# Second block, six turns between sublayers: the eight transposes of the second token tile in one group instead of two groups of four

## The reference

```python
def second_block(x, ...):
    for l in range(DEPTH):                                   # DEPTH = 2
        h = swiglu_ffn(rmsnorm(x, ffn1_pre_g[l]), ffn1_w_gu[l], ffn1_w_down[l])
        x = x + 0.5 * rmsnorm(h, ffn1_post_g[l])
        h = mixing_sublayer(rmsnorm(x, mix_pre_g[l]), w_in[l], ...)   # gating, pooling, attention, convolution
        x = x + rmsnorm(h, mix_post_g[l])
        h = swiglu_ffn(rmsnorm(x, ffn2_pre_g[l]), ffn2_w_gu[l], ffn2_w_down[l])
        x = x + 0.5 * rmsnorm(h, ffn2_post_g[l])
    return x

def swiglu_ffn(h, w_gu, w_down):                             # width 2816
    a, b = jnp.split(h @ w_gu, 2, axis=-1)
    return (jax.nn.silu(a) * b) @ w_down
```

## Time and profile before

| | |
|---|---|
| time of three runs, median (lowest to highest) | 1791.21 us (1790.86 to 1792.0) |
| the profiled execution: its time | 1792.04 us |
| its span, first to last instruction | 1790.3 us |
| granted TensorE clock, mean | 0.999 of full |
| PE busy | 1778.8 us, 99% of the span |
| PEld busy | 1588.6 us, 89% |
| DVE busy | 1402.9 us, 78% |
| ACT busy | 904.5 us, 51% |
| POOL busy | 219.7 us, 12% |
| read from HBM | 354.15 MB, 199 GB/s |

### The profile page before, as it was taken

One profiled execution on the slowest core, in us unless ns is written; L12 is line 12 of the kernel. 1 busy time (PEld: TensorE's weight loads), 2 busy tenths in 40 slices (PEclk: granted clock), 3 DMA queues, 4 the chain that ended last, 5 costly groups with the idle time before them and its releaser, 6 DMA issues.

```text
span 1790.3 us, 25922 instructions
## 1 busy us (share of the span) xinstructions
PE 1778.8 (99%) x10010; PEld 1588.6 (89%) x10010; DVE 1402.9 (78%) x1599; ACT 904.5 (51%) x998; POOL 219.7 (12%) x189
## 2 busy tenths in 40 slices
PE   9999999999999999999999999999999999999998
PEld 7988998889889898899898888998899898888997
DVE  7897867678869667777779987778777779987776
ACT  5564434445644444644555546444544555546443
POOL 0000000000001000000059230000000058230000
PEclk9999999999999999999999999999999999999999
DMA  9546565555556555655564556555655564555553
GB/s 315 205 157 227 188 212 209 189 215 200 187 215 222 205 196 186 214 197 194 181 204 172 183 210 217 202 196 192 223 199 197 188 203 167 186 212 205 201 197 117
DMA packets 52018, 357.43 MB, mean 200 GB/s; under 512 B 6552, under 2 KB 6688, under 8 KB 10080
## 3 DMA queue, kind: packets, MB, share of 16 engines
q1 hardware_dynamic: 47952, 341.93, 54.1%
q0 software_dynamic: 3696, 14.33, 2.7%
q10 hardware_dynamic: 288, 0.04, 0.0%
HBM read 354.15 MB, written 2.11 MB: 199 GB/s over the span
## 4 chain that ended last, share of the span: by engine, by line
PE 94%; DVE 4%; issue 1%; ACT 1%; DMA 1%; DVEq 0%; POOLq 0%; POOL 0%; SPq 0%; ACTq 0%
PE ps L245 21%; PE ps L327 13%; PE ps L335 13%; PE ps L328 13%; PE ps L251 11%; PE ps L207 3%; PE ps L208 3%; PE ps L209 3%; PE ps L225 2%; PE ps L232 2%; PE ps L226 2%; DVE w_lo L182 1%; PE ps L2917 1%; PE ps L2916 1%; PE ps L2921 1%
## 5 line engine op out<-in xcount | busy, mean ns | idle before, releaser
L182 DVE TENSOR_TENSOR w_lo<-raw,w_hi 128x2048 fp32r<-128x2048 f32 x312 | 717.4, 2305 | 208.4 <-ACT w_hi L175 208.0
L175 ACT ACTIVATE w_hi<-raw 128x2048 fp32r<-128x2048 f32 x312 | 596.1, 1912 | 424.1 <-PE ps L335 168.6
L245 PE MATMUL ps<-a,w_hi 128*128 128x512 f32 x1760 | 398.3, 379 | 0.8 <-ACT w_hi L175 0.8
L245 PEld LDWEIGHTS ps<-a,w_hi 128*128 128x128 f32 x1760 | 329.3, 189 | 46.0 <-ACT w_hi L175 1.2
L327 PE MATMUL ps<-w_hi,a 128*128 128x512 f32 x592 | 226.9, 383 | 0.0
L328 PE MATMUL ps<-w_hi,a 128*128 128x512 f32 x592 | 224.4, 379 | 0.0
L251 PEld LDWEIGHTS ps<-a,w_lo 128*128 128x128 f32 x1760 | 213.6, 192 | 5.9
L327 PE MATMUL ps<-w_hi,mix 128*128 128x512 f32 x576 | 218.7, 380 | 0.0
L328 PE MATMUL ps<-w_hi,mix 128*128 128x512 f32 x576 | 218.3, 379 | 0.0
L251 PE MATMUL ps<-a,w_lo 128*128 128x256 f32 x1760 | 214.2, 275 | 0.0
L335 PE MATMUL ps<-w_lo,a 128*128 128x512 f32 x592 | 139.8, 379 | 0.0
(11 more groups left out here) (416 smaller groups left out, 2267.2 us busy)
## 6 DMA issues: line engine op xcount, KB each, us to landing
raw<-in_w_b SPq DMA_DIRECT2D x198, 1024.0 KB, 4.9
raw<-in_w_a SPq DMA_DIRECT2D x124, 1024.0 KB, 4.9
rows<-in_post_gains POOLq DMA_DIRECT2D x6, 512.0 KB, 5.9
rows<-in_rows_a POOLq DMA_DIRECT2D x2, 1028.0 KB, 8.3
raw<-in_w_a SPq DMA_DIRECT2D x4, 512.0 KB, 7.1
rows<-in_rows_a POOLq DMA_DIRECT2D x2, 1024.0 KB, 6.9
x<-in_x SPq DMA_DIRECT2D x2, 512.0 KB, 6.0
a_gates<-bias_line POOLq DMA_DIRECT2D x2, 512.0 KB, 7.7
```

Source lines behind the costliest of these rows:

```text
L175: act.activation(k.w_hi[s], k.raw[:, s, :], ACT.Copy).then_inc(k.hi_ready, 1)
L182: dve.tensor_tensor(k.w_lo[s], k.raw[:, s, :], k.w_hi[s].bitcast(F32), ALU.subtract).then_inc(k.lo_ready, 1)
L245: pe.matmul(both, hi[:, kt, n * P:(n + 1) * P], k.a[:, :, kt, :].rearrange("p s (t n) -> p s n t", t=TT), start=kt == 0, stop=False)
```

## The change

At each turn the four blocks of the second half of the tile's transposes join the first four, and all eight stand behind the last product of tile 0:

```diff
@@ mlp @@
-                first_unit(1, 0, range(3))
-                x_transpose(l, n, 1, range(1))
-                first_unit(1, 0, range(3, 4)).then_inc(up0_done.sem, 1)
-                x_transpose(l, n, 1, range(1, 2))
+                first_unit(1, 0, range(4)).then_inc(up0_done.sem, 1)
+                x_transpose(l, n, 1)
                 first_unit(0, 1, range(4)).then_inc(k.chunk_done, 1)
@@ mixing sublayer @@
-                uv_part(1, 0, range(3))
-                x_transpose(l, 1, 1, range(1))
-                uv_part(1, 0, range(3, 4)).then_inc(uv_done.sem, 1)
-                x_transpose(l, 1, 1, range(1, 2))
+                uv_part(1, 0, range(4)).then_inc(uv_done.sem, 1)
+                x_transpose(l, 1, 1)
                 uv_part(0, 1, range(4)).then_inc(k.chunk_done, 1)
```

## The result

The changed kernel takes 1794.58 us, the kernel before beside it 1791.36 us, each the median of 22 runs: a ratio of 1.0019, interval [1.0013, 1.0025], or +3.2 us with an interval of +2.3 to +4.5. Forecast were 1795.1 us and +3.9 us. The interval leaves out zero, so the changed kernel is slower, by some 0.2%.

A forecast was written before the change was run, and what follows sets the result against it. PE was taken as the bound (94% of the chain), with the first transposes heading each turn's chain. Six turns x 0.65 us gave +3.9 us on the median 1791.21, so 1795.1 us; range 1793.3 to 1796.2.

The forecast's parts named there:

- ACT's 14.2 us: Sign: over all turns, ACT's waits for tile 1's transposes rise from 10.3 to 14.2 us.
- the 2.8 us in 10 waits for x: Sign: PEld's waits for x over all turns shrink from 3.7 us in 15 waits to some 2.8 us in 10.
- DVE's idle time before `x_low`: Sign in the second turn: it stays at 0.53 us or less; zero would mean DVE was the bound.
- one product per turn, 0.65 us: Each of six turns: one product moves in front of the first transposes, so the chain starts 0.65 us later.
- Wait for x worth nothing: In five turns PEld's 0.18 us wait for `x_new` goes, but gains 0; bounds 0 and 0.18 us a turn.
- no cost per group: At each turn, eight transposes in one group take as long as two groups of four; none saved.
- Rival 1: Exposed weight load of the transposes, 0.14 us, comes back in five turns: +3.2 us, 1794.4 us; chance 0.09.
- rival 2: Something the turn does not move sets the mixing sublayer's end, swallowing two turns' delay: +2.6 us, 1793.8 us; chance 0.12.
- the step at a mixing sublayer: Sign of rival 2: later turns' start shifts of 0.65, 1.3, 1.95, 2.6, 3.25 us would show a step there.
- Rival 3: At the turns DVE's last addition of x heads the chain, so not slower: -0.9 us, 1790.3 us; chance 0.03.
- Rival 4: Dearer: PE's clock falls in the turns, 1822 us, or mixing sublayer weight loads slow, up to 1796.2; chance 0.08.
- The fifth: At the turns a late second half of `x_new` splits the transposes' group again, only adding to the forecast; chance 0.02.

The follow-up runs named there:

- experiment 4: Changed kernel plus three spare 512-column matmuls in front of the eight transposes of each turn; 1799.02 us, 1.0048 of the kernel before.
- experiment 3: Changed kernel plus three spare 512-column matmuls behind the eight transposes of each turn; 1794.98 us, 1.0023 of the kernel before.
- before_b: The kernel before, unchanged, a second execution to see the scatter; 1792.44 us.
- before_c: The kernel before, unchanged, a third execution to see the scatter; 1793.17 us.
- fill_before: Kernel before plus three spare 512-column matmuls behind the second group of four transposes of each turn; 1792.51 us, 1.0007 of the kernel before.
- early: Kernel before with the first group of four transposes one product earlier, the second where it was; 1793.85 us, 1.0016 of the kernel before.
- head_early: Kernel before with DVE adding tile 1's first x half sooner and the first four transposes 0.43 us earlier; 1790.37 us, 0.9997 of the kernel before.
- head_early_b: The kernel of head_early run again, for a narrower interval; 1791.34 us, 0.9995 of the kernel before.
- late_split: experiment 2: changed kernel with two groups of four transposes, both behind tile 0's last product, two blocks' products of tile 1 between; 1803.78 us.
- after_again: The changed kernel, unchanged, run again beside others on their chip; 1794.97 us, 1.0023 of the kernel before.
- after_c: The changed kernel, unchanged, a third execution; 1794.54 us.
- g_ahead: experiment 1: changed kernel with all eight transposes in one group in front of tile 0's last product instead of behind it; 1790.67 us.
- fill_behind: experiment 3: changed kernel plus three spare matmuls behind each turn's eight transposes; 1794.98 us.
- fill_front: experiment 4: changed kernel plus three spare matmuls in front of each turn's eight transposes; 1799.02 us.
- experiment 1: Changed kernel with all eight transposes in one group, but in front of tile 0's last product; 1790.67 us, 0.9998 of the kernel before.
- experiment 2: Changed kernel with two groups of four transposes, both behind tile 0's last product, two blocks' products of tile 1 between; 1803.78 us, 1.0071 of the kernel before.

## Why the prediction was right, and where it was not exact

**The mechanism held link by link.** Forecast for the second turn were the transposes at 890.16, ACT at 890.58, DVE at 891.24, the product at 891.90; found were 890.14, 890.56, 891.22 and 891.88. That these agree to 0.02 us is luck. The forecast times leave out the delay that the first turn hands on (the prediction itself adds it elsewhere, as a shift of 0.65 us at the start of the second turn), and this execution's first stack happened to be 0.6 us shorter. The distances (1.74 us, idle 0.94 us) are the test, and they hold in each turn. ACT's 14.2 us and the 2.8 us in 10 waits for x came as written. One sign was stated wrongly: DVE's idle time before `x_low` was to stay at 0.53 us or less, but a later head lengthens it too, and it is 1.17 us in the second turn.

**The term "one product per turn, 0.65 us".** Right: 0.60 to 0.66 us in the four quiet columns, and doubled to 1.24 to 1.30 us when three more matmuls stood in front (experiment 4). The first turn is 0.05 us under it, and its chain of waits shows why: it runs through the eight evictions of ACT, which take 2.17 us in one group instead of 2.23.

**Wait for x worth nothing, no cost per group.** Both right. Rival 1, the exposed weight load, would have made 0.5 us a turn; the quiet columns behind three of the five turns concerned (3 to 4, 4 to 5, 6 to end) say 0.64 to 0.66. With it goes what the Trainium skill's rule on loads pulled ahead would give here ("TensorE: Matmul & The Clock Gate", section "What happens when you issue a matmul"). The rule itself is seen at work in experiment 3, where three loads take 0.52 us under 0.89 us of matmuls. The total alone would have misled: rival 1's 1794.4 us is nearer to the measured 1794.58 than the forecast's 1795.1, but by what happened in column 2 to 3, told next.

**Swallowed later (rival 2): its sign appeared, its mechanism did not.** Measured are +3.2 and +3.8 us, forecast +3.9. Column 5 to 6 grew by 0.57 us in the mean of three executions, but column 2 to 3 by -0.03 (188.21 to 188.18), where 0.65 was forecast. That is the step at a mixing sublayer by which the prediction would have known rival 2. Two further events of PEld divide this column: A, where it starts the weights of the attention scores (L2866), and B, where it starts those of the attention output (L2885). The lines of the kernel before, then of the changed kernel:

```profile
942.16 1.39 PEld L2866 LDWEIGHTS ps<-b_qkF 64*128 64x128 f32 x16 [0.33 <-issue]
...
983.72 0.42 PEld L2825 LDWEIGHTS ps<-consts,RL 128*128 128x128 f32 x4 [1.16 <-DVE RL L2532]
...
987.76 1.34 PEld L2885 LDWEIGHTS ps<-GU,b_v_tok 128*64 128x64 f32 x24 [0.33 <-issue]
```

```profile
942.78 1.39 PEld L2862 LDWEIGHTS ps<-b_qkF 64*128 64x128 f32 x16 [0.33 <-issue]
...
983.67 0.42 PEld L2821 LDWEIGHTS ps<-consts,RL 128*128 128x128 f32 x4 [0.49 <-DVE RL L2532]
...
987.71 1.34 PEld L2881 LDWEIGHTS ps<-GU,b_v_tok 128*64 128x64 f32 x24 [0.33 <-issue]
```

At A the changed kernel is late by 0.65 us, counted from the event in the second turn (887.47 and 887.45). Between A and B PEld waits for DVE's normalising of the attention weights (L2532, in two parts), and that wait is shorter. In all traces, us, worked out from such lines:

```
                turn to A   A to B   B to next turn   PEld's wait for L2532
before            54.69     45.60        87.93            1.16
before_b          54.67     45.38        87.93            0.55
before_c          54.67     45.65        88.10            1.21
fill_before       55.02     45.79        88.09            1.34
early             55.00     44.97        87.95            0.53
head_early        54.45     45.65        87.94            1.21
head_early_b      54.44     45.77        88.12            1.33
late_split        56.70     45.60        88.09            1.15
after             55.33     44.93        88.10            0.49
after_again       55.33     44.97        88.12            0.53
after_c           55.38     44.46        87.91            none
g_ahead           54.69     44.46        87.69            none
fill_behind       55.35     44.46        87.71            none
fill_front        55.98     44.46        87.59            none
```

Up to A every kernel shows the delay or gain of its own turn in full. From A to B 44.46 us is the floor, and PE's wait for DVE (in `before_b` with a second one of 0.52 us, for a low split) comes on top: 1.08 us in the mean of before, 0.33 us in the mean of the changed kernel. So +0.67 us in front of A, -0.76 us between A and B and about +0.06 us behind B make the column's near zero. It is not what rival 2 describes, something that the turn does not move: such a thing would make A to B shorter by as much as A is late. But `late_split`, 2.0 us late, takes the same 45.60 us as `before`, and `g_ahead`, not late at all, the same 44.46 us as `fill_front`, 1.3 us late. The wait does not follow the delay.

It goes rather with the form of the group. The six traces with all eight transposes in one group have 44.46 to 44.97 us from A to B, the eight with two groups of four 44.97 to 45.79. At the same place in the second layer that is much weaker: eleven of the fourteen traces have 44.45 or 44.46 us, three of kernels with two groups 44.85 to 44.95. DVE does its part in the first layer in different times. In the kernel before a 128x2048 split takes 3.25 us that takes 2.30 us in `g_ahead`, where the next one is the slow one:

```profile
939.35 3.25 DVE L182 TENSOR_TENSOR w_lo<-raw,w_hi 128x2048 fp32r<-128x2048 f32 x1
...
946.67 2.29 DVE L182 TENSOR_TENSOR w_lo<-raw,w_hi 128x2048 fp32r<-128x2048 f32 x1
```

```profile
938.50 2.30 DVE L182 TENSOR_TENSOR w_lo<-raw,w_hi 128x2048 fp32r<-128x2048 f32 x1
...
944.87 3.28 DVE L182 TENSOR_TENSOR w_lo<-raw,w_hi 128x2048 fp32r<-128x2048 f32 x1
```

In the kernel before one more split follows that takes 3.36 us (at 978.81), between those two parts; in `g_ahead` none does. Why a split is slow, and whether the form of the group decides it or these fourteen traces only fell so, was not tried. What the forecast lacks is therefore a term for DVE's part of the mixing sublayer, about -0.76 us by three traces against three; that this is an effect of the change is not shown.

**The rest.** Rival 3 fell: DVE was idle for 1.17 us before ACT's first part, far from being the bound. Rival 4 fell: the clock stayed at 1.00 in the turns, and no quiet column grew by more than 0.66 us. The fifth fell, too: the eight transposes' loads stand in one record, with no wait between them.

**The sum against one execution.** The profiled spans differ by 2.6 us only (1790.3, 1792.9): the six columns of these two traces add up to +3.2 us, and 0.6 us less lies in front of the first turn, where nothing was changed. One difference there is that PE waited 1.2 us for the first load of x in one trace and 0.4 us in the other.

```profile
6.25 1.07 PE L1321 MATMUL ps<-consts,x 128*128 128x128 f32 x8 [1.21 <-DMA x<-in_x]
```

```profile
5.42 1.76 PE L1321 MATMUL ps<-consts,x 128*128 128x128 f32 x8 [0.37 <-DMA x<-in_x]
```

## What to carry to other kernels

Where an engine goes idle at a seam, find the instruction that starts the chain it waits for, and place that instruction by when its input is there; independent work belongs behind it, not in front. The idle time in brackets before the waiting instruction is what may be added behind the head for nothing, and what is put in front of the head is paid, once per seam, in full where nothing behind the seam takes it up (here 0.60 to 0.66 us for 0.65 in the quiet columns). To check changes under the scatter of a whole execution, cut the traces at the same event in each seam: stretches of 175 us repeated within 0.05 us here, where whole executions scatter by a microsecond. Where such a stretch does not repeat, cut it again at events inside it before you call a delay swallowed.

## What the runs showed of the hardware that was not expected

- Eight transposes in a row and two groups of four cost PE the same (quiet columns within 0.04 us in experiment 1), and an idle time of 0.7 us on PE left the granted clock at 1.00.
- The same 128x2048 subtraction on DVE took 2.3 us mostly and longer, up to 3.41 us, in one to three places of the mixing sublayer, not the same ones in every trace. POOL was at work beside slow and fast ones alike (in the kernel before two instructions of POOL ran from 945.72 for 3.94 us, beside a split of 2.29 us), so that alone does not explain it.
- The late second group in experiment 2 cost more through ACT than on PE itself: behind the first turn PE waited 2.3 us, instead of 0.8, for a split that stood behind the late evictions.
